# A hybrid attention, mLSTM and SwiGLU block on one core: order of the attention stage's vector and scalar work, the bank of the row sums, and two orders in the gated stage

## What is computed

```python
p = rms_norm(x, g_mix) @ w_in            # aq, ak, av, and the mLSTM's columns
aq = rms_norm(aq per head of 64, q_norm_gain); ak = rms_norm(ak per head, k_norm_gain)
scores = q . k * 64 ** -0.5 + bias       # bias = -slope(head) * |distance|, window of 128 keys
probs = softmax(concat(scores, sink))[..., :-1]; att = probs @ v
mix = concat(rms_norm(att, g_attn_out), rms_norm(mlstm, g_mlstm_out))
x = x + mix @ w_out
x = x + (silu(h2 @ w_gate) * (h2 @ w_up)) @ w_down     # h2 = rms_norm(x, g_ffn)
```

## Time and profile before

| | us |
|---|---|
| median of 3 runs | 1031.36 |
| lowest, highest | 1031.03, 1031.94 |
| profiled execution, its own time | 1031.08 |
| its span, first to last instruction | 1029.3 |
| mean granted TensorE clock | 0.998 |

### The profile page before, as it was taken

The page is one execution under the profiler, slowest core; times in us unless marked ns, Lnnn a source line. Parts: engine busy times, 40 slices in busy tenths (PEclk is TensorE's granted clock), DMA queues, the critical chain, the costliest instruction groups (busy, mean ns, idle before and its releaser), DMA issues.

```text
span 1029.3 us, 13449 instructions
## 1 busy us (share of the span) xinstructions
PE 1008.7 (98%) x4970; PEld 831.9 (81%) x4970; DVE 654.4 (64%) x775; ACT 440.5 (43%) x912; POOL 691.2 (67%) x543
## 2 busy tenths in 40 slices
PE   8999999999989999989999999999999999999998
PEld 7898788877878887878888888878888888888887
DVE  4259425548862578674848686674857676574585
ACT  7545135556740656523434243433434243433440
POOL 0128668816565515968778688778778688688792
PEclk9999999999999999999999999999999999999999
DMA  7223202140032002111211211211211211211213
GB/s 232 62 60 83 83 28 75 54 143 32 21 113 70 24 5 78 52 41 42 83 41 42 82 41 43 81 41 41 82 42 42 82 41 41 82 41 42 75 63 138
DMA packets 71161, 66.06 MB, mean 64 GB/s; under 512 B 5304, under 2 KB 53688, under 8 KB 71096
## 3 DMA queue, kind: packets, MB, share of 16 engines
q1 hardware_dynamic: 70104, 64.71, 20.3%
q10 hardware_dynamic: 992, 0.49, 0.2%
HBM read 60.48 MB, written 4.21 MB: 63 GB/s over the span
## 4 chain that ended last, share of the span: by engine, by line
PE 77%; DVE 16%; issue 4%; ACT 2%; DMA 0%; SPq 0%; DVEq 0%; ACTq 0%
PE banks L805 24%; PE banks L807 23%; PE banks L806 23%; DVE af_lo L2040 8%; DVE af_raw L2032 2%; DVE af_raw L2030 2%; PE banks L825 1%; DVE sg L2016 1%; DVE af_raw L2035 1%; ACT prob L1499 1%; PE banks L999 1%; PE banks L896 1%; DVE af_raw L2019 1%; PE banks L974 1%; DMA w_raw<-in_w_in 0%
## 5 line engine op out<-in xcount | busy, mean ns | idle before, releaser
L733 POOL TENSOR_TENSOR wr_lo<-wr_raw,wr_hi 128x512 fp32r<-128x512 f32 x231 | 321.5, 1420 | 27.6 <-ACT wr_hi L1319 22.5
L727 POOL TENSOR_TENSOR wr_raw<-wr_raw,wr_raw 128x512 f32<-128x512 f32 x132 | 191.1, 1452 | 145.9 <-PE banks L807 111.0
L805 PE MATMUL banks<-hf_hi,wr_hi 128*128 128x512 f32 x616 | 242.4, 394 | 6.2 <-DVE sg L2016 4.5
L807 PE MATMUL banks<-hf_hi,wr_lo 128*128 128x512 f32 x616 | 241.0, 391 | 0.0
L806 PE MATMUL banks<-hf_lo,wr_hi 128*128 128x512 f32 x616 | 240.9, 391 | 0.0
L1319 ACT ACTIVATE wr_hi<-wr_raw 128x512 fp32r<-128x512 f32 x231 | 136.5, 624 | 166.5 <-POOL wr_raw L727 108.3
L2117 DVE TENSOR_TENSOR x<-banks,x 128x1024 f32<-128x1024 f32 x138 | 168.8, 1224 | 59.1 <-PE banks L807 45.4
L805 PE MATMUL banks<-w_hi,actT_hi 128*128 128x512 f32 (+1 forms) x448 | 173.1, 386 | 1.0 <-DVE w_lo L1710 1.0
L807 PE MATMUL banks<-w_hi,actT_lo 128*128 128x512 f32 (+1 forms) x448 | 168.2, 376 | 0.0
L806 PE MATMUL banks<-w_lo,actT_hi 128*128 128x512 f32 (+1 forms) x448 | 167.9, 375 | 0.0
L805 PEld LDWEIGHTS banks<-hf_hi,wr_hi 128*128 128x128 f32 x616 | 115.9, 188 | 35.2 <-DVE sg L2016 9.3
(11 more groups left out here) (202 smaller groups left out, 1196.9 us busy)
## 6 DMA issues: line engine op xcount, KB each, us to landing
wr_raw<-in_w_up SPq DMA_DIRECT2D x46, 256.0 KB, 3.3
wr_raw<-in_w_gate SPq DMA_DIRECT2D x44, 256.0 KB, 3.3
wr_raw<-in_w_down SPq DMA_DIRECT2D x44, 256.0 KB, 3.2
w_raw<-in_w_in SPq DMA_DIRECT2D x32, 256.0 KB, 3.5
w_raw<-in_w_out SPq DMA_DIRECT2D x16, 256.0 KB, 2.6
x<-in_x SPq DMA_DIRECT2D x8, 512.0 KB, 6.6
out<-x SPq DMA_DIRECT2D x16, 256.0 KB, 2.1
x_in<-in_x SPq DMA_DIRECT2D x7, 512.0 KB, 4.3
```

The costliest lines, as they stand in the source:

```text
L727: nc.gpsimd.tensor_tensor(wr_raw[slot(q, f)][:, :], wr_raw[slot(q, a)][:, :], wr_raw[slot(q, b)][:, :], ALU.subtract).then_inc(wsum, 1)
L733: nc.gpsimd.tensor_tensor(wr_lo[s][:, :], wr_raw[s][:, :], wr_hi[s][:, :].bitcast(F32), ALU.subtract).then_inc(wf_lo, 1)
L805: nc.tensor.matmul(ps, x_hi, wh, start=first, stop=False, skip_group_check=more)
L807: return nc.tensor.matmul(ps, x_lo, wh, start=False, stop=last, skip_group_check=more)
```

## The change

It does the following.

1. ScalarE no longer makes the scaled copy aq. VectorE multiplies the inverse root by the row's scale (`qscale`, a new instruction of 8 elements) and makes qn straight from the unit's bank. A unit's bank is free with `qn_ready`; the first output unit waits for all eight.
2. At the seam ScalarE takes the query squares ahead of the last mLSTM tile's squares, and VectorE sums them (`query_stats`) ahead of its work on that tile.
3. In a step, VectorE's order becomes: probabilities (copy, row sums, normalisation), for the output units between both additions; query sum; bias additions; maxima; query scale and product; low part of mh; copy of the row sum; low part of the attention result. ScalarE takes query square and inverse root earlier, the high part of mh behind the square.
4. The row sum goes to bank 7, and `att_sumsq` stands behind the values. The transposes of mh no longer wait for its copy; the probability transposes do, from the third tile on.
5. In the gated stage GpSimd makes block 1's differences in the order of the other blocks, ahead of its low parts; `dve_gate` puts the last `act_low` behind the addition into sg[4]; `dve_first` puts the low part of form 4 ahead of its addition.

```diff
+        qscale, _ = place("qscale", [P, 8])
...
-        aq0, e = place("aq0", [P, N], at=e)
-        aq1, e = place("aq1", [P, N], at=e)
...
-            if q == 1:
-                return 4 * q + {5: 1, 6: 2, 4: 3, 7: 4}[f]
...
-                    pool.wait_ge(wsum, sum_count(q, 5))
...
-                    block_sum(q, 4, 4, 6)
-                    pool.wait_ge(wsum, sum_count(q, 4))
-                    block_low(q, 6)
-                    block_low(q, 5)
-                    block_sum(q, 7, 3, 7)
-                    pool.wait_ge(wsum, sum_count(q, 7))
-                    for f in FORMS[4:]:
-                        block_low(q, f)
...
+                pool.wait_ge(wsum, 4 * q + 1)
+                pool.wait_ge(b22_s[q % 2], n)
+                block_sum(q, 6, 3, 5)
+                pool.wait_ge(wsum, 4 * q + 2)
+                block_sum(q, 7, 3, 7)
+                if q == 1:
+                    pool.wait_ge(b21_again, 16)
+                    block_sum(q, 4, 4, 6)
+                else:
...
+                pool.wait_ge(wsum, 4 * q + 4)
+                for f in FORMS[2:]:
+                    block_low(q, f)
...
                 ps = bank[U % 2][:, 0:width]
-                if U >= 2:
+                if U >= 4 * T + 2:
+                    pe.wait_ge(qn_ready, U - 4 * T - 1)
+                elif U >= 2:
                     pe.wait_ge(acc_free[U % 2], U // 2)
...
                     pe.wait_ge(ssa_ready, t)
-                pe.wait_ge(mixb_ready, min(t + 4, T))
-                nc.tensor.matmul(bank[3][:, 0:1], sqb[:, 0:P], ones[:, 0:1], start=True,
+                pe.wait_ge(pTd, min(t + 2, T))
+                nc.tensor.matmul(bank[7][:, 0:1], sqb[:, 0:P], ones[:, 0:1], start=True,
                                  stop=True).then_inc(ssa_mm, 1)
...
                     pe.wait_ge(mixb_ready, t)
-                if t >= 4:
-                    pe.wait_ge(ssa_ready, t - 3)
                 for kk in range(4):
...
             def att_prob_transposes(t):
+                if t >= 2:
+                    pe.wait_ge(ssa_ready, t - 1)
                 for kv in range(KV):
...
                     if j == 0:
-                        pe.wait_ge(acc_free[part], UNITS // 2)
+                        pe.wait_ge(qn_ready, T)
                     else:
                         pe.wait_ge((wa_free, x1_ready)[part], j)
...
-                if 0 <= s - 5 < T:
-                    att_sumsq(s - 5)
                 if 0 <= s - 1 < T:
                     att_transposes(s - 1)
                 if 0 <= s - 2 < T:
                     att_scores(s - 2)
                 if 0 <= s - 4 < T:
                     att_values(s - 4)
+                if 0 <= s - 5 < T:
+                    att_sumsq(s - 5)
...
-                    if t == 0:
-                        act.wait_ge(num_done, T)
                     if t >= 1:
                         act.wait_ge(q_stat, t)
-                    step(nc.scalar.activation(pq[:, :], ps[:, :], ACT.Square, scale=r_))
-                    if t >= 2:
-                        act.wait_ge(qn_ready, t - 1)
-                    nc.scalar.activation(aqs[t % 2][:, :], ps[:, :], ACT.Copy, scale=r_).then_inc(free, 1)
+                    nc.scalar.activation(pq[:, :], ps[:, :], ACT.Square, scale=r_).then_inc(pq_ready, 1)
...
+            def state_squares(t):
...
+                nc.scalar.activation(msq[:, :], mh[:, t, :], ACT.Square,
+                                     accum_out=ss2[:, t, 1:2]).then_inc(ssb_done, 1)
...
+                if 1 <= s < T:
+                    state_squares(s - 1)
...
                                          ACT.Copy, scale=cols[:, G_Q:G_Q + 1]).then_inc(qT_ready, 1)
+                if 0 <= s < T:
+                    evacuate(U)
+                if s == 0:
+                    state_squares(T - 1)
+                if 0 <= s - 1 < T:
+                    tt = s - 1
                     act.wait_ge(mh_tp, tt + 1)
                     nc.scalar.activation(actT_hi[:, tt // 4, 4:8, tt % 4 * P:(tt % 4 + 1) * P],
                                          bank[3][:, :].rearrange("p (k n) -> p k n", k=4),
                                          ACT.Copy).then_inc(mixb_hi, 1)
                 if 0 <= s < T:
-                    evacuate(U)
+                    act.wait_ge(q_stat, s + 1)
+                    if s >= 1:
+                        act.wait_ge(q_scale, s)
+                    inverse_root(qrs[:, :], qss[:, :], HD).then_inc(q_rs, 1)
...
-                if 0 <= s < T:
-                    act.wait_ge(q_stat, s + 1)
-                    if s >= 1:
-                        act.wait_ge(qn_ready, s)
-                    inverse_root(qrs[:, :], qss[:, :], HD).then_inc(q_rs, 1)
...
+            def query_stats(t):
...
+                V_.tensor_reduce(qss[:, :], pq[:, :].rearrange("p (h d) -> p h d", h=HEADS), AX.X,
+                                 ALU.add).then_inc(q_stat, 1)
...
+            def probabilities(s):
...
+                    V_.tensor_copy(pT[tt % 2][:, 4:8, :],
+                                   bank[7][:, :].rearrange("p (k n) -> p k n", k=4)).then_inc(pTd, 1)
...
+                    dve.wait_ge(p_exp, tt + 1)
+                    link(V_.tensor_tensor(dsum[:, :], dsum[:, :], esk[:, :], ALU.add))
+                    V_.reciprocal(dsum[:, :], dsum[:, :]).then_inc(p_inv, 1)
...
+                    V_.tensor_tensor(prob[tt % 2][:, 4:8, :], prob[tt % 2][:, 4:8, :], bcast(dsum[:, 4:8], P),
+                                     ALU.mult).then_inc(p_ready[1], 1)
...
+                if U == 4 * T:
+                    query_stats(0)
                 s = U - 3 * T
...
                                             ALU.add).then_inc(wa_free, 1)
+                    if j < T:
+                        probabilities(U - 4 * T)
...
                 s = U - 4 * T
-                if 0 <= s - 5 < T:
-                    tt = s - 5
-                    dve.wait_ge(ssa_mm, tt + 1)
-                    V_.tensor_copy(ss2[:, tt, 0:1], bank[3][:, 0:1]).then_inc(ssa_ready, 1)
...
-                if 0 <= s - 1 < T:
-                    tt = s - 1
-                    dve.wait_ge(mixb_hi, tt + 1)
-                    a = slice(tt % 4 * P, (tt % 4 + 1) * P)
-                    V_.tensor_tensor(actT_lo[:, tt // 4, 4:8, a],
-                                     bank[3][:, :].rearrange("p (k n) -> p k n", k=4),
-                                     actT_hi[:, tt // 4, 4:8, a].bitcast(F32),
-                                     ALU.subtract).then_inc(mixb_ready, 1)
+                if U < UNITS:
+                    probabilities(s)
+                if 1 <= s < T:
+                    query_stats(s)
...
                     steps[0] += 1
-                if 0 <= s < T:
-                    dve.wait_ge(acc_free[U % 2], U // 2 + 1)
...
-                    V_.tensor_reduce(qss[:, :], pq[:, :].rearrange("p (h d) -> p h d", h=HEADS), AX.X,
-                                     ALU.add).then_inc(q_stat, 1)
...
+                    V_.tensor_scalar(qscale[:, :], qrs[:, :], rstd[:, s:s + 1], None, ALU.mult).then_inc(q_scale, 1)
+                    dve.wait_ge(q_scale, s + 1)
...
                     V_.tensor_tensor(qn[:, :, :, :].rearrange("p i g d -> p g i d"),
-                                     aqs[s % 2][:, :].rearrange("p (g i d) -> p g i d", g=KV, i=4),
-                                     bcast(qrs[:, :].rearrange("p (g i) -> p g i", g=KV), HD),
+                                     bank[U % 2][:, :].rearrange("p (g i d) -> p g i d", g=KV, i=4),
+                                     bcast(qscale[:, :].rearrange("p (g i) -> p g i", g=KV), HD),
                                      ALU.mult).then_inc(qn_ready, 1)
+                if 0 <= s - 1 < T:
+                    tt = s - 1
+                    dve.wait_ge(mixb_hi, tt + 1)
+                    a = slice(tt % 4 * P, (tt % 4 + 1) * P)
+                    V_.tensor_tensor(actT_lo[:, tt // 4, 4:8, a],
+                                     bank[3][:, :].rearrange("p (k n) -> p k n", k=4),
+                                     actT_hi[:, tt // 4, 4:8, a].bitcast(F32),
+                                     ALU.subtract).then_inc(mixb_ready, 1)
+                if 0 <= s - 5 < T:
+                    tt = s - 5
+                    dve.wait_ge(ssa_mm, tt + 1)
+                    V_.tensor_copy(ss2[:, tt, 0:1], bank[7][:, 0:1]).then_inc(ssa_ready, 1)
...
                 if j >= 1:
-                    for f in FORMS[1:]:
+                    for f in FORMS[1:-1]:
                         act_low(j - 1, f)
                 dve.wait_ge(copied, 3 * g + 3)
                 add_product(sg[4], bank[4], 7 * g + 5)
+                if j >= 1:
+                    act_low(j - 1, FORMS[-1])
                 add_product(sg[2], bank[6], 7 * g + 6)
...
                 form_low(3, slice(0, 4 * P), 6)
+                form_low(4, slice(0, 4 * P), 7)
                 dve.wait_ge(copied, copy_of(0, 2))
```

(39 more changed lines are left out.)

34 lines of the change are left out of this document (4 added, 30 removed).

## The result

| | before | after |
|---|---|---|
| median of 4 runs each, us | 1031.65 | 1025.49 |
| profiled execution, us | 1031.08 | 1026.16 |
| its span | 1029.3 | 1024.4 |
| mean granted TensorE clock | 0.998 | 0.996 |

The ratio is 0.9943, with a 95% interval from 0.9927 to 0.996: the change is faster by 0.6%, where 1030.5 us and a range from 1027.8 to 1033.5 were predicted.

The account below looks back on a forecast made before the run. TensorE, busy 1008.7 of 1029.3 us, was taken as the bound, so only its waits could be won: 1031.08 + 2.8 (attention) - 4.9 (gated stage) + 1.6 (clock) = 1030.6, rounded to 1030.5 us; range 1027.8 to 1033.5.

Parts of the forecast that it names:

- the sum of the gated stage: Gated stage: new VectorE and GpSimd orders shorten TensorE's stalls, -4.9 us in sum, trace rows allowing -3 to -6.
- First two blocks: Gated stage: 0.5 us net at form 4, 1.6 off the stall of 3.15, 1.6 from the clock staying up.
- 676: Gated stage, stall at 676.06 (1.33 us): covered by a low part of 1.5, so 1.3 us won.
- The attention part: Attention stage: 8.5 us of waits added, 5.7 gone, net +2.8 (bounds -1 and +5); a clock fall charged at 1.6.
- seam: Before the attention stage: query squares and sum run earlier, so TensorE's whole wait of 1.44 us goes (bounds 1.0 to 1.44).
- output units: Attention stage: probabilities copied ahead of the second bank's addition, so waits of 0.42 and twice 1.51 us go.
- The first values: Attention stage, wait of 1.49 us at the first values: earlier exponentials win 0.4 us (bounds 0 and 1.49).
- What comes: Attention stage: new waits of 3.1 and 1.3 us on the copied row sum, 3.5 at the first output unit, 0.6 later.
- the clock falls twice: Rival, attention stage: the clock also falls after the stall of 3.1 us, 1.6 more, 1032.1 us; chance 0.17.
- hidden waits: Rival, attention stage: VectorE's iteration is faster than added up, only the wait for all products stays, 1024.0 us; chance 0.10.
- held scale: Rival, attention stage: GpSimd holds the new query scale, a second more in each of three long stalls, 1033.5 us; chance 0.10.
- gated stage keeps its waits: Rival, gated stage: GpSimd's new order holds VectorE's low parts as long as before, 1035.5 us; chance 0.06.

Follow-up runs that it names:

- e3: Kernel before with only the change's gated-stage orders, tiles at their old addresses: 1025.18 us, ratio 0.9942.
- e8: Kernel before with the change's gated-stage orders and 32 unused bytes, nothing of the attention part: 1018.56 us, ratio 0.9878.
- e9: Kernel before with 32 unused bytes and one low part moved behind the addition into sg[4] in each later gate block: 1020.51 us, ratio 0.9904.
- e4: Changed kernel with VectorE's copy of the row sum moved to right behind the bias additions: 1021.67 us, ratio 0.9908.
- e5: Changed kernel in which each half of the first output unit waits only for its own bank: 1020.98 us, ratio 0.9903.
- e6: Changed kernel with both the early copy of the row sum and the separate wait for each bank: 1016.35 us, ratio 0.9854.
- e2: Changed kernel with `qscale` placed in free room elsewhere, so all other tiles keep their old addresses: 1028.31 us, ratio 0.997.
- e12: Changed kernel with 128 unused bytes behind its new tile: 1028.12 us, ratio 0.9963.
- e10: Kernel before with 32 unused bytes, the first gate block's new orders and GpSimd's, later blocks' low parts as before: 1026.75 us, ratio 0.9964.
- e1: Kernel before with an unused tile of 32 bytes where the change puts its new one: 1028.83 us, ratio 0.9978.
- e7: Changed kernel with the gated stage's old orders put back: 1034.87 us, ratio 1.0044.
- e13: Changed kernel with 64 unused bytes behind its new tile: 1028.06 us, ratio 0.9966.

## Why the prediction was wrong

**The step that failed** is the sum of the gated stage: "-4.9 (trace rows allow -3 to -6)". It was -10.9. The parts, measured without the addresses by before against e3 (605.57 to 598.55, 7.0 us) and with them by e3 against e8 (3.9):

- *First two blocks* (0.5, 1.6 and 1.6 were predicted, 3.7 in all): from 381.30 to the end of the second block e3 wins 2.3. The clock stayed up in the trace, but the stall kept 2.29 of its 3.15 where 1.55 was forecast, and the first block's 1.15 became 0.28 and 0.66. The low part moved was priced rightly; in e3 the first instruction of VectorE's `act_sums` took 1.83 us where it had taken 1.34, and its five low parts 8.27 where e9's took 7.98. In the changed kernel that first instruction took 0.78, and these blocks win 4.0.
- *676*: 1.3 predicted; in e3 that block became 1.6 shorter.
- *The hidden waits*: not in the sum. 0.38 us in each of eight later blocks makes 3.1. I costed the low part's move only where a row had a bracket. The edit acts in all ten slices.
- *The addresses*: not in the sum either, 3.9 us. Of a new tile of 8 elements I priced the instruction alone.

3.7 + 1.3 = 5.0 (4.9 on record); 2.3 + 1.6 + 3.1 + 3.9 = 10.9. The blocks that the prediction went through are thus right in size, 4.0 for 3.7 in the changed kernel and 1.8 for 1.3; what failed is that it put nothing down for the rest of the stage, which wins 5.2.

**The attention part** was forecast at +2.8 and +1.6 for the clock, 4.4 in all, and came to 6.4 with the 0.6 that was lost ahead of it.

- *What goes*: seam 1.44, transposes 0.46, output units 0.42 and twice 1.51, all as predicted. The first values kept 1.21 of 1.49, so 0.3 for 0.4. Sum 5.6 for 5.7.
- *What comes*: 2.67 for 3.1, 1.18 for 1.3, 3.59 for 3.5, and no short ones for 0.6; sum 7.4 for 8.5. TensorE resumed at the copy's end, as the row of 255.71 shows. e4, e5 and e6 show both causes.
- *The clock*: this is the rival "the clock falls twice", put at 0.17. I read a threshold between 3.1 and 3.15 us out of a single fall, and it fell after 2.67. 3.1 us for 1.6.
- -5.6 + 7.4 + 3.1 = 4.9, and 0.6 ahead of it; 0.9 are left. A listed stall is shorter than the delay it makes: from matmul start to matmul start the three new waits are 2.9, 1.4 and 3.7, 0.6 more than listed, and what goes is 5.8, 0.2 more. The last 0.5 lie in gaps of under 0.3 that no list shows and that I haven't traced.

With the right clock the attention part and the gated stage as I had it would have given 1032 to 1033; it was a gain twice as big in the other stage that made the kernel faster. Errors of opposite sign met there. The *hidden waits* rival (1024.0) is nearest to the measured time and was wrong in its mechanism: the three attention waits all came. It also left out the 1.6 of clock that the prediction charges for the very stall of 3.5 that it keeps. The *held scale* and the *gated stage keeps its waits* didn't happen.

**The small instructions.** The exponentials didn't come earlier by what the bias additions moved, as argued: counted from the query transposes they start after 7.4 us in both kernels (248.11 to 255.53 before, 246.75 to 254.16 after), since the first instruction of 8 elements took 0.74 in place of 0.36 and again ended just past the same instruction of GpSimd's. The product from PSUM takes 0.69 us at 254.50 as priced. The new scale took 0.23 us six times and 0.43 in the two steps in which it ran beside GpSimd's addition of squares, so it was never held for the second that the rival needed.

## What to carry to other kernels

Where an order in a repeated block changes, measure start to start in one undisturbed repetition, not only where a wait is listed, and multiply: eight gaps of a third of a microsecond were worth 3.1 us, as much as the longest listed stall lasted. A tile added in the middle of a list moves all behind it; keep the old addresses, or compare with an unused tile of the same size in the old kernel, before a gain is put down to the edit. And part of a wait that is taken away reappears at the next one of the same loop, here 1.8 of 3.85 us and 1.2 of 3.59: mend such waits together, as e6 does, and expect cheaper work in between to count in full only when they are gone.

## What the runs showed of the hardware

**Matmul and tile address.** Twelve matmuls of 128x512 took 2.72 us with all operand tiles at the same place modulo 256 bytes, and up to 2.80 where some stood elsewhere (at four other distances); three steps took 0.68 us against 0.70.

**VectorE beside GpSimd.** The first instruction of `act_sums` in the second gate block, one and the same instruction of 128x512 from SBUF to SBUF, took from 0.69 us (e2, e12) to 1.83 (e3) with GpSimd's low parts beside it, and TensorE's stall some 18 us later moved with it: 0.66 for 0.66 between e10 and e1, 1.07 for 1.01 between e3 and e8.

**The clock falls on no fixed length of stall.** It went to its lower level, 1.2 GHz (granted 0.50 to 0.68 over the second microsecond after the stall), after stalls of 1.83 (e9), 2.65, 2.67, 2.68 (e7), 2.70, 2.85 and all of 3.14 to 5.05 us, and stayed at 2.4 GHz after 2.29, 2.32, 2.58 and 2.68 (e13). The last is the same place in the code and nearly the same length as in e12, whose rows of TensorE's timeline stand first, e13's second:

```profile
255.33 1.09 PE L968 MATMUL banks<-ident,prob 128*128 128x128 f32 x8 [2.70 <-DVE ss L2002]
256.18 0.48 PE L797 MATMUL banks<-w_hi,actT_hi 128*128 128x512 f32 x1
256.49 0.50 PE L798 MATMUL banks<-w_lo,actT_hi 128*128 128x512 f32 x1
256.80 0.63 PE L799 MATMUL banks<-w_hi,actT_lo 128*128 128x512 f32 x1
```

```profile
254.29 1.09 PE L968 MATMUL banks<-ident,prob 128*128 128x128 f32 x8 [2.68 <-DVE ss L2002]
255.14 0.47 PE L797 MATMUL banks<-w_hi,actT_hi 128*128 128x512 f32 x1
255.46 0.39 PE L798 MATMUL banks<-w_lo,actT_hi 128*128 128x512 f32 x1
```

In e12 the matmuls behind the transposes lengthen to 0.63, in e13 they go back to 0.39. One and the same kernel differs by such a fall between executions: of the kernel before's 57 executions beside the experiments, 43 had a mean granted clock of 0.998, like the profiled one, and took 1031.2 us on average; six had 1.000 and took 1029.8, eight 0.997 and 1032.6. Two of e3's four were at 1.000 (1024.02 and 1024.48) and two at 0.998 (1025.88 and 1026.4), so its trace without a fall speaks for half of them; of e9's four only the profiled one, the slowest, was below 1.000. A single trace with a stall of 1.8 to 2.9 us doesn't tell whether the clock falls at it, and a difference of 1.5 us between two kernels can be such a fall.
